# Hybrid encoder on one core: the first mixer's instruction order rewritten, M1 built on VectorE, states kept in x's words

## Chip, cores and metric

The kernel is written by hand in Bass and runs on one core of a Trainium2 chip. The metric is the device time of one execution in microseconds (us). Every buffer's place, every semaphore and the order of the instructions on each engine stand in the program; no scheduler changes them. A program on one core has one instruction stream for each of TensorE (PE), VectorE (DVE), ScalarE (ACT), GpSimd (POOL) and SyncE (SP); SP issues most DMAs.

## The reference

An encoder of two layers on x of 512 tokens by 1024 features, float32. Each layer is `x += mixer(RMSNorm(x)); x += HierMoE(RMSNorm(x))`. The change touches the mixer of layer 0, which runs two head groups from one input projection:

```python
z = (h @ w_in)
q, k, v, g, u = jnp.split(z, [512, 1024, 1536, 2048], axis=-1)
...
r = bidirectional_retention(q, k, v, decay_logit)      # 4 heads of 128, chunks of 128
...
y_ret = jax.nn.silu(g) * group_norm(r)
y_s5 = s5_glu(u, a_re, a_im, log_step, b_re, b_im, c_re, c_im, d_skip, w_glu, b_glu)
return jnp.concatenate([y_ret, y_s5], axis=-1) @ w_out
```

`s5_glu` is a diagonal state space in both directions: 32 channel groups of 16 channels, each with 64 complex states. For each group and direction, x_t = lambda x_(t-1) + B u_t, then y = d u + Re(C x) summed over the directions; then y = gelu(y), and y times sigmoid(y @ w_glu + b_glu). The mixer of layer 1 is windowed attention. HierMoE picks two of 32 experts for each token; each expert's weights are 6 MB, and all 32 are loaded in each layer.

## The kernel before

**Buffers.** `ring` has six slots of 4096 words a partition. In the expert stages slots 0 to 2 and 3 to 5 hold gate, up and down of two experts by turns; in the first mixer they hold pieces of `w_in`, tables of the state model (slots 3 to 5, from `V0`), the Toeplitz operand `TQ` (slot 1), the transposed operands `T4` of the retention (slot 2), and at the end the halves of `w_out`. `WK` ("work") holds q, k, v, g, u and small arrays, `HT` the normed input transposed and later scratch, `X` ("x_sb") the residual. PSUM has eight banks.

**The state model without a scan over tokens.** The 512 tokens are 64 chunks of 8 (`T8`, `NK`). `dve_s5_params` (L1107) computes lambda and its powers, `dve_s5_tables` (L1176) C times the powers of lambda and B for the convolution kernel inside a chunk, `dve_phasors` (L1207) the 64 powers of lambda^8's phase, by doubling: n values times the n-th power give the next n, and after each doubling that power is squared. `pool_m1` (L1382) multiplies, on GpSimd, B by powers of lambda for a quarter q of the groups (`M1`, 128 x 2048). `pe_m1` and `act_m1` transpose it to `W1S`, `pe_inc` (L1415) makes the chunk increments from it and u, `act_inc` copies them to SBUF, and `dve_states` (L1441) rotates them by the phasors, runs two scans over the 64 chunks, rotates back and writes the states of the quarter. `pe_y` (L1477) adds, in PSUM, the Toeplitz product inside the chunk and C times the states; `act_gelu` evacuates. All products of complex numbers go through `cmul` (L984 to L1000), six instructions each.

**Order in the program** (one sequence an engine, written out in `pe_mixer0` L1525, `act_mixer0` L1653, `dve_mixer0` L1717, `sp_mixer0` L1774). TensorE: norm transposes, u (64 x 512 for each of 8 token phases), transposes of C and of u, `z_block` (L1551) for q, k and g in four banks, kernel products (L1588), v, then the whole retention `pe_ret` (L1272), then `pe_m1`, `pe_inc`, `pe_y` interleaved by quarters, transposes of y (L1613), GLU products (L1624) with the transposes of the retention result between them, output projection (L1641, L1645). VectorE: `dve_small_logs` (L1055, decay logarithms and the masks of the retention), parameters, tables, phasors, `dve_kernel` (L1225), `dve_rotary` (L1240), `dve_ret`, four `dve_states`, `dve_gn` (L1354), the rest. GpSimd: small loads, then the four `pool_m1` behind `z_mm` 12. SP: x, pieces of `w_in`, small loads (s5_d in one transfer, L1785), the kernel stored to DRAM and loaded as `TQ` (L1812), `w_out`, and then `sp_moe` (L819), which loads expert weights as slots come free; its first loads wait for `yr_rdy`, `gl_mm`, and `o_mm` 4 and 8 (the output projection's halves).

## Time and profile before

| what | us |
|---|---|
| median of 3 runs (lowest, highest) | 1731.51 (1729.74, 1734.15) |
| the profiled execution: its time, its span | 1726.8, 1725.0 |
| TensorE busy | 1407.0 (82%) |
| VectorE busy | 539.9 (31%) |
| ScalarE busy | 246.3 (14%) |
| GpSimd busy | 230.0 (13%) |
| HBM read, written | 465.92 MB, 23.59 MB |

Busy time is summed over the span. The pages' slices are equal parts of the span, 43 us each; the stage tables below give the same by stretches of my choosing. In the timelines the first number is the start, the second the duration, and in brackets stands how long the engine sat idle before and who released it.

### The profile page before, as it was taken

The numbers are of one execution on the slowest core, as the hardware profiler recorded it, in microseconds if no ns is written. First come the engines' busy times: TensorE is split into PE (matmuls) and PEld (weight loads), VectorE is DVE, ScalarE is ACT, GpSimd is POOL, SyncE is SP. The second block draws the span as 40 slices with busy tenths as digits, with TensorE's granted clock in tenths as the row PEclk, the third lists the DMA queues.
The fourth block names the chain that finished last, engine by engine and source line by source line (L and its number), as shares of the span: only waits on it lengthen the run. The fifth ranks groups of instructions, "written<-read, shape, count | busy, mean of one in ns | idle before, by whom it ended". The sixth has DMA issues, their size and how long they took to land. (4 is left out here: it accounts for less than half of the span.)

```text
span 1725.0 us, 18834 instructions
## 1 busy us (share of the span) xinstructions
PE 1407.0 (82%) x7013; PEld 686.9 (40%) x7013; DVE 539.9 (31%) x1251; ACT 246.3 (14%) x529; POOL 230.0 (13%) x330
## 2 busy tenths in 40 slices
PE   7998746997988878878884988896997887887882
PEld 4444645555333333333332356544433333333330
DVE  6998589123111111110114039524111011011014
ACT  3101222111100000000011027412000000000001
POOL 0007070001111111111100000001111111111110
PEclk9999977996998998998996989996999999899896
DMA  7210502536999999999996110426999999999994
GB/s 241 71 52 21 45 13 84 213 151 236 365 397 411 404 410 412 407 406 409 400 407 248 54 49 2 195 85 228 341 384 410 408 407 406 409 405 411 406 419 160
DMA packets 70724, 473.49 MB, mean 274 GB/s; under 512 B 16676, under 2 KB 23556, under 8 KB 45968
## 3 DMA queue, kind: packets, MB, share of 16 engines
q1 hardware_dynamic: 57872, 448.07, 66.5%
q0 software_dynamic: 11376, 19.83, 3.5%
q10 hardware_dynamic: 1424, 4.89, 0.7%
q8 instruction: 34, 0.56, 0.1%
q14 instruction: 18, 0.15, 0.0%
HBM read 465.92 MB, written 23.59 MB: 284 GB/s over the span
## 5 line engine op out<-in xcount | busy, mean ns | idle before, releaser
L616 PE MATMUL psum<-ring,work 128*64 128x512 f32 x992 | 494.1, 656 | 117.2 <-DMA ring<-in_moe_w_up 115.7
L617 PE MATMUL psum<-ring,work 128*64 128x512 f32 x992 | 494.9, 657 | 0.0
L616 PEld LDWEIGHTS psum<-ring,work 128*64 128x64 f32 x992 | 144.9, 151 | 430.8 <-issue 427.1
L629 PE MATMUL psum<-ring,work 128*64 128x512 f32 x992 | 226.5, 598 | 31.1 <-DVE work L761 31.1
L758 DVE TENSOR_TENSOR work<-work,psum 64x512 f32<-64x512 f32 x64 | 44.2, 690 | 597.2 <-ACT work L722 597.1
L722 ACT ACTIVATE work<-psum 64x512 f32<-64x512 f32 x64 | 37.8, 590 | 833.6 <-PE psum L617 833.6
L617 PEld LDWEIGHTS psum<-ring,work 128*64 128x64 f32 x992 | 144.7, 151 | 2.5 <-issue 1.0
L629 PEld LDWEIGHTS psum<-ring,work 128*64 128x64 f32 x992 | 66.6, 136 | 144.9 <-issue 125.1
L764 DVE COPY work<-psum 128x512 f32<-128x512 f32 x64 | 44.2, 691 | 247.7 <-PE psum L629 247.7
L1562 PE MATMUL psum<-ring,hT 128*128 128x512 f32 x256 | 112.1, 600 | 2.1 <-ACT work L1685 2.1
L902 POOL COPY ints<-ints 64x1 uint32 (+1 forms) x64 | 11.4, 178 | 538.3 <-PE psum L608 499.4
L1562 PEld LDWEIGHTS psum<-ring,hT 128*128 128x128 f32 x256 | 49.1, 193 | 63.7 <-issue 63.7
L920 POOL DMA_INDIRECT y_dram<-work,ints x64 | 65.3, 1020 | 56.7 <-POOL ints L926 55.6
L909 POOL DMA_INDIRECT work<-h_dram,ints x64 | 61.8, 966 | 58.2 <-POOL ints L902 54.2
L608 PE MATMUL psum<-consts,work 64*128 64x64 f32 x512 | 67.3, 273 | 2.8 <-DMA work<-h_dram,ints 2.8
L608 PEld LDWEIGHTS psum<-consts,work 64*128 64x128 f32 x512 | 62.7, 204 | 4.7 <-DMA work<-h_dram,ints 3.1
L1934 PE MATMUL psum<-ring,hT 128*128 128x512 f32 x128 | 55.6, 593 | 0.7 <-ACT hT L1971 0.7
L622 PEld LDWEIGHTS psum<-consts,work 64*128 64x128 f32 x256 | 35.4, 209 | 51.9 <-issue 51.9
L1853 PE MATMUL psum<-hT,ring 128*64 128x512 f32 x256 | 55.2, 592 | 0.8 <-issue 0.8
L312 PE MATMUL psum<-consts,work 128*128 128x128 f32 x128 | 25.7, 367 | 33.4 <-DVE work L281 33.4
L719 ACT COPY work<-psum 128x512 f32<-128x512 f32 x64 | 37.4, 585 | 75.9 <-PE psum L608 75.9
L622 PE MATMUL psum<-consts,work 64*128 64x64 f32 x256 | 44.1, 292 | 0.0
(362 smaller groups left out, 1450.9 us busy)
## 6 DMA issues: line engine op xcount, KB each, us to landing
ring<-in_moe_w_gate SPq DMA_DIRECT2D x62, 2048.0 KB, 17.5
ring<-in_moe_w_up SPq DMA_DIRECT2D x62, 2048.0 KB, 22.9
ring<-in_moe_w_down SPq DMA_DIRECT2D x62, 2048.0 KB, 23.3
ring<-in_hyb_w_in SPq DMA_DIRECT2D x5, 2048.0 KB, 8.6
work<-y_dram SPq DMA_DIRECT2D x16, 512.0 KB, 7.2
ring<-in_swa_w_qkv SPq DMA_DIRECT2D x3, 2048.0 KB, 15.0
ring<-in_hyb_w_out SPq DMA_DIRECT2D x4, 1024.0 KB, 8.7
h_dram<-work ACTq DMA_DIRECT2D x8, 512.0 KB, 2.6
```

The source lines that it names most:

```text
L608: i = nc.tensor.transpose(bank[b][:, c * BLK:(c + 1) * BLK], XG[b][:, c::KC], ident[0:BLK, 0:BLK])
L616: nc.tensor.matmul(bank[2 + b][0:BLK, :], XT[b][:, c, :], g[:, c, :], start=c == 0, stop=c == KC - 1)
L617: i = nc.tensor.matmul(bank[2 + b][BLK:P, :], XT[b][:, c, :], u[:, c, :], start=c == 0, stop=c == KC - 1)
L622: i = nc.tensor.transpose(bank[4 + b][:, c * BLK:(c + 1) * BLK], HD[b][:, c::HC], ident[0:BLK, 0:BLK])
L629: i = nc.tensor.matmul(bank[6 + b][BLK * hf:BLK * (hf + 1), :], HTE[b][:, c, :], d[:, c, hf * HALF:(hf + 1) * HALF], start=c == 0, stop=c ...
L758: nc.vector.tensor_tensor(HD[b], AA[b], bank[2 + b][BLK:P, :], ALU.mult).then_inc(done, 1)
L764: nc.vector.tensor_copy(YE[b], bank[6 + b][:, :]).then_inc(done, 1)
L909: pool.indirect_dma_start(XG[b], None, h_dram, bass.IndirectOffsetOnAxis(STG[b], 0), bounds_check=S - 1, oob_is_err=False).then_inc(done, 16)
L920: pool.indirect_dma_start(y_dram, bass.IndirectOffsetOnAxis(SSTG[b], 0), YE[b], None, bounds_check=4 * S - 1, oob_is_err=False).then_inc(d ...
L1562: x = nc.tensor.matmul(bank[i % 4], hT[:, c, t * P:(t + 1) * P], w[:, c, :], start=c == 0, stop=c == KC - 1)
L1853: x = nc.tensor.matmul(bank[i][64 * hf:64 * hf + 64, :], w[:, c, 64 * (2 * k + hf):64 * (2 * k + hf) + 64], hT[:, c, :], start=c == 0, sto ...
L1934: x = nc.tensor.matmul(b, hT[:, c, t * P:(t + 1) * P], wo[n][:, c, :], start=c == 0, stop=c == KC - 1)
```

## The change

It rewrites the order of the first mixer on all engines, and with it:

- M1 is built on VectorE (`dve_m1`, in place of `pool_m1`), two quarters right behind the parameters and two later; quarter 0 lies in WK, the others in slot 0, and `W1S` in slot 0 too.
- Transposes of M1 (by halves, in banks 2 and 3), increments and kernel products stand between the tiles of q, k, v, g, which use two banks instead of four; v comes before g.
- `act_inc` is gone: VectorE reads the increments from PSUM. The states of all four quarters are kept, in the words of x (`XS`), so x is loaded a second time from DRAM before the output projection adds to it.
- `dve_phasors` takes the n-th power from the table itself, so the six squarings fall away. Small logs move behind the last states.
- y runs after all states in one stretch, ahead of the retention; the retention stands behind y, and the GLU products behind it, before the transposes of the retention result.
- Channel groups g and g + 16 share the two halves of the partitions, instead of 2j and 2j + 1. So `YT` has 128 rows and its transposes are 64 products with a quarter of the identity, s5_d comes in eight small loads, the parameter rows on GpSimd's queue in six instead of three.
- The expert weights' first loads wait for the same points, with other slots: slots 3 to 5 at `yr_rdy`, 0 at `gl_mm`, 1 and 2 at the projection's halves.

The core of the diff:

```diff
-        T4 = W(2, 2048, 2048)
-        M1 = [W(0, 2048 * b, 2048) for b in range(2)]
-        W1S = cut(WK, 4096, 2048)
+        T4, YT = W(2, 0, 2048), W(2, 2048, 2048)
+        M1 = [cut(WK, 2048, 2048)] + [W(0, 0, 2048)] * (NQ - 1)
+        W1S = W(0, 2048, 2048)
...
+        XS = [[cut(X, 1024 * q + 512 * i, 512) for i in range(2)] for q in range(NQ)]
...
             while n < NK:
-                bc = [ins_dim(m(x), 2, n) for x in ("qr", "qi")]
-                cmul(V, p3[0][:, :, n:2 * n], p3[1][:, :, n:2 * n], p3[0][:, :, 0:n], p3[1][:, :, 0:n], bc[0], bc[1],
-                     shp(cut(RR, 0, 32 * n), 32, n), shp(cut(RR, 1024, 32 * n), 32, n))
-                cmul(V, m("t3"), m("t4"), m("qr"), m("qi"), m("qr"), m("qi"), m("t1"), m("t2"))
-                V(tv.tensor_copy(m("qr", 2), m("t3", 2)))
-                V.sync()
+                w = min(n, NK - 1 - n)
+                bc = [ins_dim(x[:, :, n], 2, w) for x in p3]
+                cmul(V, p3[0][:, :, n + 1:n + 1 + w], p3[1][:, :, n + 1:n + 1 + w], p3[0][:, :, 1:1 + w], p3[1][:, :, 1:1 + w],
+                     bc[0], bc[1], shp(cut(RR, 0, 32 * w), 32, w), shp(cut(RR, 1024, 32 * w), 32, w))
                 n *= 2
...
-        def pool_m1(pool, V, q):
+        def dve_m1(dve, V, q):
 
             if q == 0:
-                pool.wait_ge(z_mm.s, 12)
-            elif q > 1:
-                pool.wait_ge(m1_tr.s, 4 * (q - 1))
+                dve.wait_ge(b_in, B_LOADS)
+            elif q == 1:
+                dve.wait_ge(u_mm.s, 4)
+            else:
+                dve.wait_ge(m1_tr.s, 4 * q)
...
         def dve_states(dve, V, q):
 
-            dve.wait_ge(inc_ev.s, 2 * q + 2)
-            if q >= 2:
-                dve.wait_ge(y_mm.s, 2 * (q - 1))
+            dve.wait_ge(inc_mm.s, 2 * q + 2)
...
+            def kernel_products():
+                pe.wait_ge(k_tab.s, 1)
+                pe.wait_ge(m1_ev.s, 8)
...
+            z_tile(0)
+            pe_m1(pe, 0, 0)
+            z_tile(1)
+            pe_m1(pe, 0, 1)
+            z_tile(2)
+            pe_inc(pe, 0)
...
+            z_tile(6)
+            kernel_products()
+            z_tile(7)
...
+            z_tile(15)
...
             for q in range(NQ):
+                pe_y(pe, q)
...
+            pe_ret_transposes(pe, 0)
             pe.wait_ge(y_ge.s, 2 * NQ)
             for mm in range(4):
                 for t in range(T8):
-                    x = nc.tensor.transpose(bank[4 + mm][:, t * 64:(t + 1) * 64], YT[:, 512 * t + mm:512 * t + 512:4],
-                                            ident[0:64, 0:64])
+                    for gg in range(2):
+                        rows = slice(64 * gg, 64 * gg + 64)
+                        x = nc.tensor.matmul(bank[4 + mm][rows, t * 64:(t + 1) * 64], YT[rows, 256 * t + mm:256 * t + 256:4],
+                                             ident[rows, rows], start=True, stop=True)
...
+            dve_s5_params(dve, V)
+            dve_m1(dve, V, 0)
+            dve_m1(dve, V, 1)
+            dve_phasors(dve, V)
+            dve_s5_tables(dve, V)
+            dve_states(dve, V, 0)
+            dve_kernel(dve, V)
+            dve_m1(dve, V, 2)
+            dve_states(dve, V, 1)
+            dve_m1(dve, V, 3)
+            dve_states(dve, V, 2)
+            dve_rotary(dve, V)
+            dve_states(dve, V, 3)
             dve_small_logs(V)
...
+            for j in range(QJ):
+                for gg in range(2):
+                    r0 = 32 * j + 16 * gg
+                    sp.dma_start(SMP[r0:r0 + GC, 4:8], bass.AP(A["s5_d"].tensor, 256 * gg + GC * j, [[1, GC], [QJ * GC, NQ], [1, 1]]),
+                                 allow_slow_non_contiguous=True).then_inc(b_in, 16)
...
             sp.wait_ge(y_mm.s, 2 * NQ)
+            for t in range(NT):
+                sp.dma_start(xv[:, t, :], A["x"][0, t * P:(t + 1) * P, :]).then_inc(x_in[t], 16)
+            wout(0)
+            sp.wait_ge(ym_tr.s, 4)
+            sp.wait_ge(r_o.s, RH)
+            wout(1)
```

How the order moves. TensorE around the kernel products, before (`s5_tables` is raised by VectorE behind the tables, `z_evac` by ScalarE; L1562 is a tile of q, k, g or v):

```order
L1562 MATMUL psum<-ring,hT 128x512 [waits z_evac]
L1562 MATMUL psum<-ring,hT 128x512 x7
L1588 MATMUL psum<-ring,work 32x128 [waits s5_tables,u_ready]
L1588 MATMUL psum<-ring,work 32x128 x63
L1562 MATMUL psum<-ring,hT 128x512 [waits z_evac,w_loaded1]
L1562 MATMUL psum<-ring,hT 128x512 x7
```

and now (L1569 is a tile, L1593 the kernel products, L1416 a half of M1's transposes):

```order
L1569 MATMUL psum<-ring,hT 128x512 [waits z_evac]
L1569 MATMUL psum<-ring,hT 128x512 x7
L1593 MATMUL psum<-ring,work 32x128 [waits s5_m1_evac,s5_tables]
L1593 MATMUL psum<-ring,work 32x128 x63
L1569 MATMUL psum<-ring,hT 128x512 [waits z_evac]
L1569 MATMUL psum<-ring,hT 128x512 x7
L1569 MATMUL psum<-ring,hT 128x512 [waits z_evac,w_loaded1]
L1569 MATMUL psum<-ring,hT 128x512 x7
L1569 MATMUL psum<-ring,hT 128x512 [waits z_evac]
L1569 MATMUL psum<-ring,hT 128x512 x7
L1416 MATMUL psum<-consts,ring 128x128 [waits s5_m1_evac,s5_kernel_ready,s5_m1]
L1416 MATMUL psum<-consts,ring 128x128 x7
```

Before, twelve tiles stood ahead of the kernel products; now seven do, and transposes of M1 stand between the tiles behind them.

TensorE behind the last tile, before (L1281 are the retention's transposes):

```order
L1562 MATMUL psum<-ring,hT 128x512 [waits z_evac]
L1562 MATMUL psum<-ring,hT 128x512 x7
L1281 MATMUL psum<-consts,work 128x128 [waits ret_scaled,z_evac,s5_kernel_ready]
L1281 MATMUL psum<-consts,work 128x128 x3
L1281 MATMUL psum<-consts,hT 128x128 x8
```

and now (L1630 the bias row for layer 1, L1498 the Toeplitz product of y, L1504 its product with the states):

```order
L1569 MATMUL psum<-ring,hT 128x512 [waits z_evac]
L1569 MATMUL psum<-ring,hT 128x512 x7
L1630 MATMUL psum<-work 16x512 [waits s5_m1_evac,attn_small_loaded]
L1498 MATMUL psum<-ring,work 64x128 [waits s5_toeplitz_loaded,s5_states]
L1498 MATMUL psum<-ring,work 64x128
L1504 MATMUL psum<-ring,x_sb 64x128 x8
```

y has taken the place of the retention, and its first product waits for the states of all quarters.

VectorE around the end of the tables, before (L1204 is the tables' last instruction, L1210 begins the phasors):

```order
L999 TENSOR_TENSOR ring<-work 128x576 [waits dve_steps]
L1204 MEMSET ring 128x32 [waits dve_steps]
L1210 MEMSET work 128x32 [waits u_transposed,s5_tables]
L1211 MEMSET work 128x32
L1212 COPY ring<-ring 128x32
```

and now (L1206 is the tables' last; what follows is the first state group):

```order
L1000 TENSOR_TENSOR ring<-work 128x576 [waits dve_steps]
L1206 MEMSET ring 128x32 [waits dve_steps]
L989 TENSOR_TENSOR work<-work,psum 128x512 [waits s5_inc,s5_tables]
L990 TENSOR_TENSOR work<-work,psum 128x512
L992 TENSOR_TENSOR work<-work 128x512 [waits dve_steps]
```

The phasors stand ahead of the tables now, and the states begin behind the tables, with PSUM as an input.

## Rows read from the trace of the kernel before

**Rows 1.** The page: DMA's busy tenths in 40 slices, and a group of matmuls.
```profile
DMA  7210502536999999999996110426999999999994
...
L616 PE MATMUL psum<-ring,work 128*64 128x512 f32 x992 | 494.1, 656 | 117.2 <-DMA ring<-in_moe_w_up 115.7
```
**Rows 2.** Stages: length; PE, PEld, DVE, ACT, POOL busy (instructions); clock, DMA share, GB/s.
```profile
20.03:38.78 18.75, 18.69 (x88) 8.94 (x90) 17.01 (x62) 2.32 (x4) 0.00 (x0) 1.00 0.72 191
38.78:63.10 24.32, 22.87 (x105) 11.59 (x102) 21.53 (x114) 7.60 (x13) 0.00 (x0) 0.93 0.31 108
63.10:108.50 45.40, 45.40 (x107) 20.14 (x106) 43.47 (x70) 3.55 (x6) 0.00 (x0) 1.00 0.13 47
108.50:135.20 26.70, 26.70 (x63) 11.78 (x62) 24.64 (x83) 0.60 (x1) 0.00 (x0) 1.00 0.12 40
135.20:145.06 9.86, 7.73 (x138) 5.13 (x137) 4.16 (x16) 3.35 (x5) 7.80 (x8) 1.00 0.01 2
145.06:176.55 31.49, 25.25 (x59) 10.83 (x57) 31.22 (x24) 2.34 (x4) 27.30 (x21) 0.98 0.27 40
181.80:212.65 30.85, 25.23 (x219) 24.47 (x218) 17.80 (x44) 7.00 (x15) 0.00 (x0) 0.99 0.43 34
217.35:242.95 25.60, 6.90 (x91) 6.12 (x89) 25.14 (x22) 1.92 (x4) 24.74 (x18) 0.68 0.00 1
259.50:270.86 11.36, 8.94 (x138) 6.96 (x135) 10.88 (x22) 2.95 (x6) 0.00 (x0) 0.80 0.04 13
283.50:298.50 15.00, 10.04 (x100) 8.12 (x101) 14.33 (x10) 3.96 (x5) 0.00 (x0) 0.73 0.41 142
302.30:321.20 18.90, 18.89 (x48) 12.05 (x49) 0.47 (x1) 4.00 (x7) 0.00 (x0) 0.84 0.87 365
```
**Rows 3.** Timeline of VectorE: start, us, instruction.
```profile
121.11 0.69 DVE L988 TENSOR_TENSOR work<-work,ring 128x512 f32<-128x512 f32 x1
...
125.21 0.19 DVE L988 TENSOR_TENSOR ring<-ring 128x32 f32<-128x32 f32 x1
...
126.55 1.23 DVE L988 TENSOR_TENSOR work<-work,ring 128x1024 f32<-128x1024 f32 x1
...
173.92 0.68 DVE L1252 TENSOR_TENSOR work<-work,consts 128x512 f32<-128x512 f32 x1
174.52 0.68 DVE L1253 TENSOR_TENSOR work<-work,consts 128x512 f32<-128x512 f32 x1
```
**Rows 4.** Timeline of GpSimd.
```profile
136.95 1.06 POOL L988 TENSOR_TENSOR norm_gain<-ring,work 128x512 f32<-128x512 f32 x1 [132.81 <-PE psum L1562]
...
171.86 1.59 POOL L999 TENSOR_TENSOR ring<-norm_gain 128x512 f32<-128x512 f32 x1
```
**Rows 5.** Timeline of TensorE.
```profile
52.41 84.35 PE L1562 MATMUL psum<-ring,hT 128*128 128x512 f32 x192
136.70 3.77 PE L1588 MATMUL psum<-ring,work 128*32 128x128 f32 x128
...
219.32 2.09 PE L1426 MATMUL psum<-work 128*64 128x64 f32 x64 [0.83 <-ACT work L1413]
230.94 3.67 PE L1403 MATMUL psum<-consts,ring 128*128 128x128 f32 x16 [9.53 <-POOL ring L999]
...
276.54 0.44 PE L1493 MATMUL psum<-ring,work 128*64 128x128 f32 x4
...
277.93 1.03 PE L1607 MATMUL psum<-work 32*16 32x512 f32 x2
...
296.08 4.10 PE L1613 MATMUL psum<-consts,work 64*128 64x64 f32 x32 [4.93 <-ACT work L1508]
```
**Rows 6.** Timeline of SP's DMA issues.
```profile
9.57 5.42 SPq L1785 DMA_DIRECT2D s_small<-in_s_d  x1
...
170.40 10.04 SPq L1812 DMA_DIRECT2D ring<-k_dram  x8
```
**Rows 7.** DMA issues by tile: count, KB each, median us to landing.
```profile
ring<-k_dram SPq DMA_DIRECT2D x8, 256.0 KB, 12.9
```

More of the change, by code:

```diff
@@ L43 @@
 NTAU = T8 + 1
+B_LOADS = 16 * 13
 AH = 16
@@ L817, in load_block_w, with sp_moe @@
             q.dma_start(W(3 * b + which), v).then_inc(done, 16)
-        def sp_moe(sp, l, free_s5, free_2, free_0, free_1, next_loads):
+        def sp_moe(sp, l, frees, next_loads):
             b0 = NE * l
-            for free, slots in ((free_s5, (3, 4, 5)), (free_2, (2,)), (free_0, (0,)), (free_1, (1,))):
+            for free, slots in frees:
                 free(sp)
@@ L1211, in dve_phasors @@
             V(tv.memset(p3[1][:, :, 0:1], 0.0))
-            V(tv.tensor_copy(m("qr"), m("e8r")))
-            V(tv.tensor_copy(m("qi"), m("e8i")))
+            for x, e8 in zip(p3, ("e8r", "e8i")):
+                V(tv.tensor_copy(x[:, :, 1], m(e8)))
             V.sync()
@@ new lines, in pe_mixer0 @@
+            z_tile(0)
[4 more added lines that the diff above has]
+            pe_inc(pe, 0)
+            pe_m1(pe, 1, 0)
+            z_tile(3)
+            pe_m1(pe, 1, 1)
+            z_tile(4)
+            pe_inc(pe, 1)
+            z_tile(5)
+            z_tile(6)
+            kernel_products()
+            z_tile(7)
+            z_tile(8)
+            z_tile(9)
+            pe_m1(pe, 2, 0)
+            z_tile(10)
+            pe_m1(pe, 2, 1)
@@ new lines, in pe_mixer0 @@
+            z_tile(11)
+            pe_inc(pe, 2)
+            z_tile(12)
+            pe_m1(pe, 3, 0)
+            z_tile(13)
+            pe_m1(pe, 3, 1)
+            z_tile(14)
+            pe_inc(pe, 3)
+            z_tile(15)
+            pe.wait_ge(a_in, 32)
+            pe.wait_ge(m1_ev.s, 4 * NQ)
+            nc.tensor.matmul(bank[3][0:AH, :], RB, OH[:, 0:S], start=True, stop=True).then_inc(f_mm.s, 1)
+            for q in range(NQ):
+                pe_y(pe, q)
+            pe.wait_ge(f_ev.s, 1)
@@ L1690, in act_mixer0, with z_out @@
[L1690 to L1705 removed]
+            def z_out(i):
+                _, reg = ZB[ZORD[i // NT]]
+                act.wait_ge(z_mm.s, i + 1)
+                if i == 2 * NT:
+                    act.wait_ge(k_mm.s, 2)
+                o = cut(WK, 2048 * reg + 512 * (i % NT), 512)
+                if ZORD[i // NT] == "g":
+                    A_(nc.scalar.activation(o, bank[i % 2], ACT.Silu), z_ev)
+                elif ZORD[i // NT] == "k":
+                    A_(nc.scalar.mul(o, bank[i % 2], RD ** -0.5), z_ev)
+                else:
+                    A_(nc.scalar.copy(o, bank[i % 2]), z_ev)
@@ new lines, in act_mixer0 @@
+            z_out(0)
+            act_m1(act, A_, 0, 0)
+            z_out(1)
+            act_m1(act, A_, 0, 1)
+            z_out(2)
+            act_m1(act, A_, 1, 0)
+            z_out(3)
+            act_m1(act, A_, 1, 1)
+            for i in range(4, 10):
+                z_out(i)
+            act_m1(act, A_, 2, 0)
+            z_out(10)
+            act_m1(act, A_, 2, 1)
+            z_out(11)
+            z_out(12)
+            act_m1(act, A_, 3, 0)
+            z_out(13)
+            act_m1(act, A_, 3, 1)
@@ L1706, in act_mixer0 @@
+            z_out(14)
+            act.wait_ge(k_st, 16)
+            act.dma_start(OH, A["c_band"]).then_inc(a_in, 16)
+            act.dma_start(RB, A["rel_bias"]).then_inc(a_in, 16)
+            z_out(15)
+            for q in range(NQ):
+                act_gelu(act, A_, q)
+            act_ret(act, A_)
+            act_gn(act, A_)
             for mm in range(4):
@@ L1709, in act_mixer0 @@
                    gl_sg)
-                if mm == 1:
-                    for m4 in range(4):
-                        act.wait_ge(yr_tr.s, m4 + 1)
-                        A_(nc.scalar.copy(YRT[:, 512 * m4:512 * m4 + 512], bank[4 + m4]), yr_ev)
+            for m4 in range(4):
+                act.wait_ge(yr_tr.s, m4 + 1)
+                A_(nc.scalar.copy(YRT[:, 512 * m4:512 * m4 + 512], bank[4 + m4]), yr_ev)
             act.wait_ge(f_ev.s, 1)
@@ L1762, in dve_add_out @@
                 dve.wait_ge(o_mm.s, 8 * l + i + 1)
+                if l == 0 and n == 0:
+                    dve.wait_ge(x_in[t], 32)
                 xx = xv[:, t, 512 * n:512 * n + 512]
```

335 lines of the change are left out of this document (139 added, 196 removed).

## The prediction

> **What bounds the kernel now.** I read the page first. Its slices [rows 1] show DMA at 0.9 for most of the span, in two long blocks, which are the two expert stages. There the matmuls of `pe_gu` (L616) wait 115.7 us in total for expert weights to land [rows 1]. Nothing in those stages changes except the order of the first loads, so their length stays. The blocks cannot start before the mixer ahead of each has ended, though: six ring slots hold the weights, and the mixer occupies them. In the first mixer's slices (the first nine) DMA stands at 0.0 to 0.5 after the start [rows 1]. So a microsecond taken from this mixer moves all that follows to the left by one. Its end for this purpose is the first output projection, which starts at 321.2 us, where the last stage of the table ends [rows 2].
>
> Within the mixer the stage table [rows 2] shows a relay. VectorE is full from 20 to 135 us (small logs 18.8, parameters 24.3, tables 45.4, phasors 26.7) while TensorE works on u, q, k, g. Then come rotary (31.5), retention (30.9), four groups of states, the group norm (15.0), and the GLU with the transposes of the retention result (18.9). From 176.5 us on TensorE and VectorE take turns. One thing stands out: the first group of states took 25.6 us and the third 11.4 for the same 22 instructions, and the rotary's 24 instructions took 31.2 us of VectorE. GpSimd was busy in just the slow ones (24.74 and 27.30 us, against 0.00) [rows 2]. An instruction on 128x512 takes 0.69 or 0.68 us when GpSimd is idle [rows 3]; the two at 173.92 and 174.52 follow right behind GpSimd's last one, which began at 171.86 and took 1.59 [rows 4]. The mean in the rotary was 31.22 / 24 = 1.30. The two engines slow each other.
>
> **The change, part by part.** I follow VectorE first, as it becomes the long chain. All durations are of the profiled execution.
>
> 1. Small logs leave the front: the parameters start at 20.0 instead of 38.8 and end at 20.0 + 24.3 = 44.3.
> 2. Matrix M1 moves from GpSimd to VectorE: per quarter two complex products, each of six instructions on 512 elements. One such product ran from 121.11 to 125.21, 4.1 us [rows 3], so 8.2 per quarter, 32.8 in all. Two quarters stand here: 60.7. The first waits for thirteen small loads, the second for u's matmuls; q's first tile, which stands behind those on TensorE, starts at 52.41 [rows 5], so the second doesn't wait.
> 3. Phasors lose six squarings with their copies, 126.55 - 125.21 = 1.34 each [rows 3], and one part in 32 of the last doubling (0.2): 26.7 - 8.2 = 18.5, to 79.2.
> 4. Tables 45.4: 124.6. Here TensorE waits (below).
> 5. State group 0: 11.4 [rows 2], now from PSUM instead of ScalarE's copy; same price, as no row shows more for PSUM. 136.0. The convolution kernel's 16 small instructions: 4.2, the busy time of their stage [rows 2]. 140.2. M1 of quarter 2: 148.4. State group 1: 159.8.
> 6. M1 of quarter 3 writes where TensorE still reads quarter 2, so it waits for that one's transposes, at about 162 by the count below: 170.2. State group 2 waits for its increments until about 171: 182.4.
> 7. Rotary without GpSimd beside it: 24 x 4.1 / 6 = 16.4 instead of 31.5. 198.8. State group 3: 210.2.
>
> So 190 us of VectorE, some 3 of them waits. Only M1 has no row of its own on VectorE. Bounds: below 29 (48 instructions at the 0.60 between the starts at 173.92 and 174.52 [rows 3]), above 51 (GpSimd's own 1.06 each [rows 4]). I take 32.8, from the row of the same engine and size.
>
> The Trainium skill (GPSIMD Engine Reference, Key points) calls VectorE structurally about twice as fast for elementwise work. By that, an estimate of mine, M1 would cost half of GpSimd's 51 us, 25, and the sum would be 7 us better. The rows give 0.68 against 1.06, a factor of 1.6, and the sum keeps to the rows.
>
> TensorE: the first tile starts at 52.4 as before. Twelve tiles took 84.35 us [rows 5], 7.0 each. Between them now stand sixteen transposes (half of 3.67 at full clock, 1.8) and the increment products (2.09) [rows 5] of two quarters, 8 together. After seven tiles it is at 52.4 + 49 + 8 = 109.5, where the kernel products wait for the tables: idle to 124.6, **15 us that were none before**. The wait costs nothing by itself, as VectorE is behind. But the clock falls: at 230.94, after 9.5 us idle, those transposes took 3.67 [rows 5]. So the kernel products at 3.77 [rows 5] or double, then a tile with a slow start: 139.5 after tile 7. Tiles 8 and 9, half the transposes, tile 10, the other half: 162, the time used in 6. Tiles 11 to 15 (35) with the transposes and increments of a quarter and the increments of the one before (6): 203. SP beside this: the Toeplitz loads go out behind tile 11, from 169, in 10 us [rows 6], and land 12.9 later in the median [rows 7]: by 197, before 210. w_glu, x again (2 MB) and half of w_out follow and are wanted only from 272, 297 and 290 on.
>
> Then all of y in one run: four quarters of four pieces. A piece took 277.93 - 276.54 = 1.39 at full clock [rows 5], a quarter 5.6, at half clock up to 11.1. With a slow start, 7.4 + 3 x 5.6 = 24.2: from 210.2 to 234.4. **Small logs, 18.8, stand beside it on VectorE** and end at 229.0; with the bias row and the first scaling, five instructions of at most 0.69, at 232.5: hidden, by 2 us. If y took less than 22, they would be next. Last GELU and the first head's transposes: 236. The transposes of y become 64 products instead of 32 transposes of 4.10 [rows 5]; by the increments, 32 such products in 2.09, 4.2 (bounds 2.1, and 8.4 at half clock). Last copy by VectorE: 241.2. Retention from its first increments on 30.9 [rows 2]: 272.1. Group norm 15.0: 287.1. The GLU's products (with a few transposes 18.9 [rows 2]) now run beside it, from 271.5 to 286 or 290. Last, transposes of the result 1.8 and a copy, with hand-over: 290.2. That is 321.2 - 290.2 = **31 us** earlier. ScalarE loses eight copies and has idle time everywhere; GpSimd only issues small loads.
>
> What follows (projection, router, expert stages) is equal: expert 0's gate loads earlier, but its up and down weights still wait for the projection's halves.
>
> The profiled execution's own time is 1726.8, the median 1731.51, 4.7 more: 1731.5 - 31 = **1700.5**.
>
> **The rivals.** (a) *TensorE stays slow after its waits.* This one ends on the other side. The new order cuts the projections with short transposes and waits. Where TensorE waited for VectorE between short groups, its granted clock was 0.68 (217 to 243) and 0.80 (259 to 271); with dense tiles it was 1.00 (63 to 108) [rows 2]. If it stayed at the lower level, 1.2 GHz, from 124.6 on, nine tiles would cost 7 us more each, 63, of which 7 are slack; y 17, retention and GLU some 10: 83 - 31 = 52 slower, 1783. It decides from about 38 us of slow work on, five tiles. Against it: between the short groups stand dense runs of 7 us. The Trainium skill (TensorE: Matmul & The Clock Gate, on oscillation) describes just this pattern, short groups between waits that start slow each time. A mild form, y alone slow, gives 1700.5 + 17 = 1717.5.
>
> (b) *The small loads block SP.* s5_d was one issue of 5.42 us [rows 6]; it is eight now, ahead of k's weights. At that price each they end 43 us after the B loads, near 70, land near 79, and VectorE's first M1 waits 34: 1734.5, no change. Against: that issue stood behind 4 MB of weights, and the eight together move as many elements.
>
> (c) *The slowness was not GpSimd's.* Then M1, rotary and states stay at 1.3 us an instruction: M1 +30, rotary +15, states +14: 1759.5. The rows at 173.92 and 174.52 [rows 3] speak plainly against it.
>
> (d) *It does not reach the end*, because the weight stream sets it: 1731.5. Against: DMA is hardly busy before the first block [rows 1].
>
> (e) Full clock and shorter waits everywhere: 40 us, 1691.5.
>
> **How the numbers follow.** Chances: forecast 0.76 (1693 to 1710), mild (a) 0.08, full (a) 0.05, (b) 0.04, (c) 0.02, (d) 0.01, (e) 0.04. Range 1687 to 1719: the forecast with M1's bounds (-4, +18), mild (a) and (e); 0.12 is left out. A difference of 0.3%, 5 us, is what a measurement here can tell from none. Faster 0.88, same 0.05, slower 0.07.
>
> **What would show it.** Right: no VectorE row on 128x512 much above 0.7 us in the mixer; the kernel products after a wait of 15 us near 125; the last state group done near 210; y in one run of about 24; the projection at 290, and expert stages of the old length. Wrong: granted clock near 0.5 in the tiles after 125 (a), a wait for the B loads at 44 (b), instructions of 1.3 us with GpSimd idle (c), longer expert stages (d).

## The result, and the profile after

The change made the kernel faster: 1701.13 us in the median of 4 runs (1697.05 to 1705.08), against 1730.62 (4 runs, 1728.84 to 1734.15) for the kernel before on the same chip. The ratio is 0.9833, with a 95% interval of 0.9812 to 0.9854. That is 29.5 us by the medians, or 1.7%, clear of the noise; 31 were forecast. The profiled execution took 1700.29 us, its span 1698.4.

The page of the changed kernel, to be held against [rows 1]: the slices of DMA's busy tenths, and the group of matmuls that waits for expert weights.

```profile
DMA  8012533458999999999984200436999999999994
...
L617 PE MATMUL psum<-ring,work 128*64 128x512 f32 x992 | 488.6, 650 | 120.3 <-DMA ring<-in_moe_w_up 118.9
```

The first long block is fuller at its front (8 where a 6 stood) and ends earlier (8 where the last 9 stood). The wait for weights is 118.9 us, 3.2 more than before: the expert stages did not shrink, they moved. From the first expert matmul to the end of the span it is 1316.0 us, and was 1314.8.

The stages of the changed kernel, in the columns of [rows 2]: M1 of quarters 0 and 1, phasors, tables, state group 0, kernel taps, M1 of quarter 2, rotary, y, y transposes, retention, group norm.

```profile
44.94:61.43 16.49, 15.04 (x84) 8.15 (x81) 15.88 (x25) 4.75 (x9) 0.00 (x0) 1.00 0.00 1
61.43:80.17 18.74, 18.74 (x116) 9.92 (x115) 17.63 (x41) 3.72 (x7) 0.00 (x0) 1.00 0.00 0
80.17:125.39 45.22, 31.63 (x146) 15.57 (x144) 43.47 (x71) 4.43 (x8) 0.00 (x0) 0.88 0.14 47
125.39:136.89 11.50, 11.37 (x143) 7.71 (x144) 10.95 (x23) 0.00 (x0) 0.00 (x0) 0.86 0.01 1
136.89:140.44 3.55, 3.55 (x10) 1.63 (x9) 3.24 (x16) 0.60 (x1) 0.00 (x0) 1.00 0.34 63
140.44:148.65 8.21, 8.21 (x20) 3.61 (x19) 7.93 (x12) 0.59 (x1) 0.27 (x1) 1.00 0.82 289
180.56:196.00 15.44, 15.44 (x102) 8.20 (x101) 15.16 (x25) 2.16 (x4) 0.00 (x0) 1.00 0.69 116
207.35:232.88 25.53, 25.53 (x337) 19.40 (x337) 19.45 (x66) 5.30 (x10) 0.53 (x1) 0.94 0.10 30
232.88:241.94 9.06, 7.89 (x129) 7.75 (x129) 4.39 (x4) 1.49 (x4) 0.00 (x0) 1.00 0.95 347
241.94:272.75 30.81, 25.16 (x210) 24.25 (x211) 17.80 (x44) 7.44 (x13) 0.00 (x0) 1.00 0.08 30
272.75:287.84 15.09, 13.13 (x31) 8.95 (x30) 14.36 (x10) 4.01 (x6) 0.00 (x0) 1.00 0.39 140
```

VectorE is full in every stage down to 207. The rotary, 31.49 us in [rows 2], takes 15.44, with GpSimd at 0.00. State group 0, 25.60 before, takes 11.50. M1 costs 8.2 us a quarter. Retention and group norm have kept their lengths.

Two of VectorE's waits, and then TensorE's, in the timeline of the changed kernel (in brackets: the idle time before the instruction, and who ended it):

```profile
160.32 0.69 DVE L989 TENSOR_TENSOR norm_gain<-ring,work 128x512 f32<-128x512 f32 x1 [0.37 <-PE psum L1416]
...
169.18 0.69 DVE L989 TENSOR_TENSOR work<-work,psum 128x512 f32<-128x512 f32 x1 [0.69 <-PE psum L1440]
```
```profile
125.53 5.24 PE L1593 MATMUL psum<-ring,work 128*32 128x128 f32 x128 [13.73 <-DVE ring L1206]
...
200.62 1.03 PE L1630 MATMUL psum<-work 32*16 32x512 f32 x2
207.35 0.69 PE L1498 MATMUL psum<-ring,work 128*64 128x128 f32 x4 [5.70 <-DVE x_sb L1476]
...
232.88 7.89 PE L1642 MATMUL psum<-consts,ring 64*64 64x64 f32 x128
...
291.42 5.87 PE L1670 MATMUL psum<-ring,work 128*128 128x512 f32 x8 [0.68 <-ACT work L1751]
```

Up to y, TensorE waits for VectorE (13.73 and 5.70 us) and VectorE almost never for TensorE. The output projection starts at 291.42, 29.8 us before 321.2 [rows 2].

### The profile page after: what moved, and what is told of

It is laid out like the page before. It is cut to its first block and busy times, and to the rows that moved or that the text cites. A ratio compares the mean times of both kernels' runs of the same rounds, so it can differ in the third digit from the quotient of the medians.

```text
span 1698.4 us, 18976 instructions
## 1 busy us (share of the span) xinstructions
PE 1399.7 (82%) x7109; PEld 670.4 (39%) x7109; DVE 531.7 (31%) x1257; ACT 240.9 (14%) x520; POOL 165.5 (10%) x285
## 5 line engine op out<-in xcount | busy, mean ns | idle before, releaser
L617 PE MATMUL psum<-ring,work 128*64 128x512 f32 x992 | 488.6, 650 | 120.3 <-DMA ring<-in_moe_w_up 118.9
L1569 PE MATMUL psum<-ring,hT 128*128 128x512 f32 x256 | 112.5, 594 | 0.0
L1569 PEld LDWEIGHTS psum<-ring,hT 128*128 128x128 f32 x256 | 47.6, 190 | 55.5 <-issue 55.2
L903 POOL COPY ints<-ints 64x1 uint32 (+1 forms) x64 | 11.4, 178 | 533.5 <-PE psum L609 494.7
```

Source lines behind the costliest of these rows:

```text
L617: nc.tensor.matmul(bank[2 + b][0:BLK, :], XT[b][:, c, :], g[:, c, :], start=c == 0, stop=c == KC - 1)
L1569: x = nc.tensor.matmul(bank[i % 2], hT[:, c, t * P:(t + 1) * P], w[:, c, :], start=c == 0, stop=c == KC - 1)
```

## The experiments

Each was timed beside the kernel before on its own chip, so ratios carry over from chip to chip better than times. The changed kernel's is 0.9833, and 0.001 of a ratio is 1.7 us. Where a difference of medians and one of ratios disagree, both are given.

### 1. Is VectorE's list the path? The small logs back in front

```diff
             V.sync()
+            dve_small_logs(V)
             dve_s5_params(dve, V)
...
             dve_states(dve, V, 3)
-            dve_small_logs(V)
```

> The changed kernel with one block moved back: the small logs (decays, router mask, softplus and the scaling of the keys, 18.8 us of VectorE in the changed kernel's trace) stand ahead of the state model's parameters again. Theory (VectorE's list is the chain from the start to the retention, and the small logs are hidden beside the products of the state outputs y): every later step moves back by 18.8 us and nothing is won behind y, so about 1720 us, +18.8. Rival (TensorE and the weight loads set the end of the stage, VectorE has slack after the change): between 0 and +12 us, the latter where only the 14 us wait of TensorE at the kernel products absorbs it.

1719.81 us, ratio 0.9942 (0.9923 to 0.9960): 18.7 above the changed kernel. VectorE's last group before the retention and its next instruction in this kernel's timeline:

```profile
226.60 1.67 DVE L1268 TENSOR_SCALAR hT<-work,ring 128x512 f32<-128x512 f32 x4
...
253.56 1.10 DVE L1783 COPY work<-psum 128x512 f32<-128x512 f32 x1 [25.28 <-PE psum L1642]
```

VectorE now sits idle for 25.28 us beside y, where the small logs had been. The whole price of this block is hidden in the change, and it is paid in full in front. The 13.73 us that TensorE had waited absorbed nothing.

### 2. The squarings, back in the changed kernel and out of the one before

In the changed kernel (with the two copies that start qr and qi; the result is used by nothing):

```diff
                      bc[0], bc[1], shp(cut(RR, 0, 32 * w), 32, w), shp(cut(RR, 1024, 32 * w), 32, w))
+                cmul(V, m("t3"), m("t4"), m("qr"), m("qi"), m("qr"), m("qi"), m("t1"), m("t2"))
+                V(tv.tensor_copy(m("qr", 2), m("t3", 2)))
+                V.sync()
                 n *= 2
```

> The changed kernel with the six squarings of the phasor loop and their copies put back on VectorE; their result is used by nothing, so this adds only their time (six of 1.34 us with the two copies, about 8 us). Theory (VectorE is the chain from the start on): +8 us, about 1709. Rival (VectorE has slack before the kernel tables, since TensorE's products wait anyway): 0.

1711.68 us, ratio 0.9886 (0.9847 to 0.9926): 10.6 above the changed kernel by the medians, 9.2 by the ratios, and the projection starts 9.1 later (300.55). In the kernel before, the new loop alone:

```diff
-                bc = [ins_dim(m(x), 2, n) for x in ("qr", "qi")]
-                cmul(V, p3[0][:, :, n:2 * n], p3[1][:, :, n:2 * n], p3[0][:, :, 0:n], p3[1][:, :, 0:n], bc[0], bc[1],
+                w = min(n, NK - 1 - n)
+                bc = [ins_dim(x[:, :, n], 2, w) for x in p3]
+                cmul(V, p3[0][:, :, n + 1:n + 1 + w], p3[1][:, :, n + 1:n + 1 + w], p3[0][:, :, 1:1 + w], p3[1][:, :, 1:1 + w],
...
-                cmul(V, m("t3"), m("t4"), m("qr"), m("qi"), m("qr"), m("qi"), m("t1"), m("t2"))
-                V(tv.tensor_copy(m("qr", 2), m("t3", 2)))
```

> The kernel before with one part of the change alone: the phasor loop without its squarings, about 8 us less of VectorE ahead of the kernel tables. Theory (before the change the same instructions lie on VectorE's path too, but it waits 5.4 us for the kernel products and for the first-mixer matrices that GpSimd makes behind it): the gain is between 0 and 3 us, since GpSimd's chain of matrices starts at the end of the tables' inputs and of the tile 12 projection and not of the tables. Rival (VectorE is the chain there as well): -8 us.

1730.26 us, ratio 1.0 (0.9979 to 1.0021): nothing. VectorE in this kernel, from its timeline:

```profile
126.38 1.19 DVE L999 TENSOR_TENSOR work<-work 128x992 f32<-128x992 f32 x1
140.94 0.29 DVE L1229 COPY work<-psum 128x128 f32<-128x128 f32 x1 [13.37 <-PE psum L1586]
```

It finishes 7.6 us earlier and then waits 13.37 us for the kernel products; in the kernel before that wait is 5.43. The same edit is worth its full price in the one order and nothing in the other.

### 3. Is M1 on GpSimd the cause of the slow VectorE?

M1 on VectorE, in the kernel before and its old order:

```diff
-                cmul(V, o[:, d, 0], o[:, d, 1], gg[0], gg[1], bb[0], bb[1], t1, t2, eng=nc.gpsimd,
+                cmul(V, o[:, d, 0], o[:, d, 1], gg[0], gg[1], bb[0], bb[1], t1, t2,
...
             dve_kernel(dve, V)
+            dve_m1(dve, V, 0)
+            dve_m1(dve, V, 1)
             dve_rotary(dve, V)
             dve_ret(dve, V)
+            dve_m1(dve, V, 2)
             dve_states(dve, V, 0)
+            dve_m1(dve, V, 3)
```

> The kernel before, in its old order, with the four quarters of the first-level matrices M1 computed by VectorE and not by GpSimd, and the loads of quarter 0's router ahead of nothing: GpSimd has no arithmetic left there. Theory (GpSimd and VectorE slow each other when both run float32 tensor-tensor work from SBUF: 1.5 us for an instruction of 0.69): VectorE pays 32.8 us for M1 and gets back the rotary's doubling (15.6 us), the states' doubling (about 11) and its waits for M1 (about 14), so -8 us, about 1722. Rival (GpSimd's M1 is free for VectorE, its slow instructions come from something else): +19 to +33 us, 1750 to 1763, with VectorE's rotary still at 1.5 us an instruction.

1722.99 us, ratio 0.9951 (0.9930 to 0.9973), 5.9 below its neighbour by the medians and 8.5 by the ratio. VectorE took 33 us of work over and the kernel still got faster. The rotary's stage, in the columns of [rows 2]:

```profile
162.95:178.52 15.57, 9.85 (x23) 3.99 (x22) 15.26 (x26) 1.17 (x2) 0.00 (x0) 0.88 0.35 36
```

This is 15.57 us against 31.49 [rows 2]. The rival wanted 19 to 33 us more.

The other way round, half of M1 back on GpSimd in the changed kernel:

```diff
-                cmul(V, o[:, d, 0], o[:, d, 1], gg[0], gg[1], bb[0], bb[1], t1, t2,
-                     done=m1_rdy if d else None)
+                cmul(V, o[:, d, 0], o[:, d, 1], gg[0], gg[1], bb[0], bb[1], t1, t2, eng=nc.gpsimd if on_pool else None,
+                     done=(m1_rdp if on_pool else m1_rdy) if d else None)
...
-            dve_m1(dve, V, 2)
             dve_states(dve, V, 1)
-            dve_m1(dve, V, 3)
```

> The changed kernel with the M1 matrices of quarters 2 and 3 computed by GpSimd again, beside VectorE's kernel, states 1 and 2 and rotary; quarters 0 and 1 stay on VectorE. Theory (the two engines slow each other): VectorE is rid of two quarters (16.4 us), GpSimd needs about 24 us for each of them, and VectorE's instructions beside it go from 0.69 to about 1.5 us, so the gain is given back: about +2 us against the changed kernel, 1699 to 1707. Rival (no slowing, GpSimd's work is free): -16 us, about 1685, with VectorE's instructions beside it still at 0.69 us.

1709.41 us, ratio 0.9906 (0.9879 to 0.9934): 8.3 above the changed kernel by the medians, 12.6 by the ratios, outside what either theory gave. Quarter 2 ran beside the tables. GpSimd there, and then on the same work while VectorE sat idle; below it VectorE:

```profile
91.11 1.66 POOL L993 TENSOR_TENSOR ring<-norm_gain 128x512 f32<-128x512 f32 x1
92.85 1.45 POOL L995 TENSOR_TENSOR norm_gain<-ring,work 128x512 f32<-128x512 f32 x1
...
171.91 1.26 POOL L993 TENSOR_TENSOR ring<-norm_gain 128x512 f32<-128x512 f32 x1
173.25 1.05 POOL L995 TENSOR_TENSOR norm_gain<-ring,work 128x512 f32<-128x512 f32 x1
```
```profile
86.37 0.76 DVE L993 TENSOR_TENSOR ring<-work 128x576 f32<-128x576 f32 x1
...
91.57 1.81 DVE L991 TENSOR_TENSOR work<-work,ring 128x576 f32<-128x576 f32 x1
...
109.29 0.75 DVE L991 TENSOR_TENSOR work<-work,ring 128x576 f32<-128x576 f32 x1
...
178.64 0.69 DVE L990 TENSOR_TENSOR work<-work,psum 128x512 f32<-128x512 f32 x1 [17.53 <-PE psum L1442]
```

The slowing is there, as expected: 0.76 becomes 1.5 to 1.8. What I had missed is the last row. The slowed tables end late, so the kernel products start at 134.89 for 125.53, and all that stands behind them on TensorE is 9.4 us late as well; the increments of quarter 2 reach VectorE at 178.64 for 169.18. VectorE has no M1 left to do until then, and the 16.4 us that it saved became a wait of 17.53. TensorE's list is the second chain, close behind the first.

The pure case: the changed kernel with 24 additions on GpSimd whose result nothing uses. The wait for them in the diff is met 21.6 us before VectorE gets there (202.78 against 224.40, below).

```diff
+            pool.wait_ge(m1_rdy.s, NQ)
+            for _ in range(24):
+                Q(nc.gpsimd.tensor_tensor(PM2, PM1, PM1, ALU.add), dum)
+                Q.sync()
             pool.wait_ge(r_sc.s, 1)
...
             dve_states(dve, V, 3)
+            dve.wait_ge(dum.s, 24)
             dve_small_logs(V)
```

> The changed kernel, and on GpSimd 24 additions of 128x512 float32 in SBUF, whose result nothing uses, from the end of the last M1 quarter on: they lie beside VectorE's states of quarter 2 (the first four of whose six long multiplications read one operand from PSUM) and its rotary (24 instructions with both operands in SBUF). Nothing waits for them. Theory (the two engines slow each other whenever both work from SBUF alone): GpSimd needs about 1.5 us for each while VectorE works from SBUF and about 1.1 where it doesn't, VectorE's rotary goes from 0.69 to about 1.5 us an instruction for as long as GpSimd runs, VectorE's instructions with a PSUM operand stay at 0.69 us; VectorE loses 10 to 15 us and the kernel with it, 1711 to 1716. Rival (the slowing of the kernel before came from GpSimd's DMA issues, from its waits or from the data's place and not from its arithmetic): 0, 1701.

1719.65 us, ratio 0.9950 (0.9934 to 0.9967): 18.5 above the changed kernel by the medians, 20.2 by the ratios, a little over the top of what was expected, for additions that no one needs. GpSimd and VectorE in this kernel:

```profile
169.56 33.22 POOL L2182 TENSOR_TENSOR norm_gain<-norm_gain 128x512 f32<-128x512 f32 x24 [17.88 <-DVE ring L1001]
```
```profile
172.29 0.69 DVE L995 TENSOR_TENSOR work<-work,psum 128x512 f32<-128x512 f32 x1
...
174.85 1.15 DVE L1455 COPY work<-ring 128x512 f32<-128x512 f32 x1
...
176.17 3.72 DVE L1460 TENSOR_TENSOR_SCAN work<-work 128x512 f32<-128x512 f32 x2
...
182.76 2.32 DVE L1479 TENSOR_TENSOR x_sb<-work 128x252 f32<-128x252 f32 x2
...
201.81 1.52 DVE L1253 TENSOR_TENSOR work<-work,consts 128x512 f32<-128x512 f32 x1
203.25 0.68 DVE L1254 TENSOR_TENSOR work<-work,consts 128x512 f32<-128x512 f32 x1
...
224.40 0.17 DVE L1063 TENSOR_SCALAR work<-s_small 128x8 f32<-128x8 f32 x1
```

GpSimd's last addition ends at 202.78, and VectorE's rotary drops from 1.52 to 0.68 us at once. The small logs begin at 224.40 instead of 207.40, 17.0 late. The row at 172.29 is as telling: with one operand in PSUM the instruction took its 0.69 us beside a working GpSimd. Those with all data in SBUF paid, also the copy with its one operand (1.15 for 0.43), the two scans (3.72 for 2.34) and a pair on 252 elements (2.32 for 0.75), which is why the sum passed my 10 to 15.

The Trainium skill (SBUF — State Buffer, A bandwidth-pool intuition that's wrong (but worth ruling out)) says that GpSimd and a VectorE operation that uses both of its ports can't work at the same time: one fully blocks. The trace agrees that they collide; that an operand in PSUM escapes is what the rows above show. Each engine's instruction gets longer: GpSimd's from 1.05 to 1.45 and from 1.26 to 1.66, VectorE's from 0.69 to 1.52. Whether one stands still within its row while the other works, durations can't tell. If the whole of each took turns, a pair would need 0.69 + 1.05 = 1.74 us; here VectorE started an instruction every 1.44 us (201.81 to 203.25) beside GpSimd's 24 in 33.22, 1.38 each, so they overlap at least in part.

### 4. Does TensorE's new wait cost anything? The kernel products later

```diff
             z_tile(6)
-            kernel_products()
             z_tile(7)
             z_tile(8)
+            kernel_products()
             z_tile(9)
```

> The changed kernel with TensorE's kernel products behind the projections of tiles 7 and 8 and not ahead of them, so that the 13.7 us in which TensorE waits for VectorE's tables are filled with projections. Theory (TensorE's wait costs nothing, since the retention starts when VectorE's states and y are done): 0, within 2 us of the changed kernel's 1701. Rival (TensorE's list is a second chain nearly as long): a gain of several us, up to 14.

1700.56 us, ratio 0.9851 (0.9828 to 0.9874): no difference from the changed kernel that these can show. TensorE's two waits in this kernel:

```profile
148.79 1.97 PE L1416 MATMUL psum<-consts,ring 128*128 128x128 f32 x8 [11.97 <-DVE ring L1000]
207.12 0.69 PE L1498 MATMUL psum<-ring,work 128*64 128x128 f32 x4 [5.72 <-DVE x_sb L1476]
```

The wait has moved to the M1 transposes, 11.97 us long, and y starts at 207.12 instead of 207.35.

### 5. What made the y transposes twice as dear as forecast?

The 64 products read every fourth word of y. Here they read neighbours, so that other rows of y reach the GLU than the reference's; nothing else changes.

```diff
-                        x = nc.tensor.matmul(bank[4 + mm][rows, t * 64:(t + 1) * 64], YT[rows, 256 * t + mm:256 * t + 256:4],
+                        x = nc.tensor.matmul(bank[4 + mm][rows, t * 64:(t + 1) * 64], YT[rows, 256 * t + 64 * mm:256 * t + 64 * mm + 64],
```

> The changed kernel, in which the 64 products that transpose y read 64 neighbouring words of each row and not every fourth word (so other rows of y reach the GLU than the reference's; the count and the shape of everything stay). Theory (the step of four words in the stationary operand is why a product takes 123 ns here against 65 ns in the state increments): 64 products in about 4.2 us, VectorE's four copies of 1.1 us then set the pace, -2.5 to -3 us, 1698.5. Rival (the price is that of this shape, an identity against 64 words of 64 partitions, whatever the step): 7.9 us again, 1701.

1697.05 us, ratio 0.9783 (0.9756 to 0.9810), below the changed kernel by 4.1 in the medians and 8.7 by the ratios; 2.5 to 3 were expected. TensorE in this kernel, and then the line's weight loads in the changed one and in this one:

```profile
232.83 3.95 PE L1642 MATMUL psum<-consts,ring 64*64 64x64 f32 x128
238.04 0.94 PE L1292 MATMUL psum<-work,hT 128*128 128x128 f32 x6 [1.26 <-DVE work L1783]
```
```profile
L1642 PEld LDWEIGHTS psum<-consts,ring x128: 189/213/213, 232.9 to 240.4; 64*64 64x64 f32 x128
```
```profile
L1642 PEld LDWEIGHTS psum<-consts,ring x128: 129/135/135, 232.8 to 236.5; 64*64 64x64 f32 x128
```

3.95 us against 7.89, a load 135 ns against 213, and the retention starts 3.9 us earlier (238.04 for 241.94). The step was the price, not the shape. A step of two or of eight was not tried. The Trainium skill (SBUF — State Buffer, Door 1: The DMA port swizzle) states that SBUF delivers full bandwidth only with at least two accesses to each line of 16 bytes; a step of four float32 words makes one. The trace agrees with that sentence, though the page then counts a step of four float32 as free.

### 6. Better than both: the last states ahead of the rotary

Once VectorE is the path, what must precede y should come first, and the rotary, which only the retention needs, can lie beside y like the small logs.

```diff
-            dve_rotary(dve, V)
             dve_states(dve, V, 3)
+            dve_rotary(dve, V)
             dve_small_logs(V)
...
-            pe_m1(pe, 2, 0)
             z_tile(10)
+            pe_m1(pe, 2, 0)
             pe_m1(pe, 2, 1)
...
             pe_m1(pe, 3, 0)
-            z_tile(13)
             pe_m1(pe, 3, 1)
-            z_tile(14)
             pe_inc(pe, 3)
+            z_tile(13)
+            z_tile(14)
             z_tile(15)
...
-            pe.wait_ge(f_ev.s, 1)
-            pe.wait_ge(z_ev.s, 16)
-            pe_ret_transposes(pe, 0)
             pe.wait_ge(y_ge.s, 2 * NQ)
...
+            pe.wait_ge(f_ev.s, 1)
+            pe.wait_ge(z_ev.s, 16)
+            pe_ret_transposes(pe, 0)
             pe.wait_ge(ym_ev.s, 4)
```

The kernel products stand as in experiment 4, and ScalarE's list follows TensorE's.

> The changed kernel with the kernel products behind tiles 7 and 8, the M1 products of quarters 2 and 3 each in one piece (the last increments ahead of tile 13), the last quarter's states ahead of the rotary on VectorE, and the transposes of y ahead of the first retention transposes on TensorE: the 16 us of rotary then lie beside the products of the state outputs, as the small logs do, and the y transposes beside the rotary. Theory (the chain is VectorE's list up to the last state, then y, and VectorE idles 6.5 us plus four short waits behind the small logs): about -10 us, near 1691; the bound above is the sum of the idle time, the y chain itself (some 25 us from the last state) stays. Rival (the last states must wait for the last increments, which stand behind all projections that z of the rotary needs as well; the wait only moves): 0.

1687.87 us, ratio 0.9787 (0.9761 to 0.9814): 13 below the changed kernel by the medians, and 12.7 below experiment 4, which ran beside it, but 8 by the ratios; 10 were expected. The same kernel a second time, beside the last one of this series:

> The kernel with the states ahead of the rotary once more, unchanged, beside the other on the same chip, so that the two are compared without the difference between chips: 1688 us, a span of 1686 again, within 2 us.

1689.81 us, ratio 0.9754 (0.9727 to 0.9782). So the gain over the changed kernel is 8 to 14 us. The timelines of the first of the two show VectorE's copies of y without a wait between them, and TensorE reaching the y transposes and then the retention with hardly a pause:

```profile
225.74 1.68 DVE L1268 TENSOR_SCALAR hT<-work,ring 128x512 f32<-128x512 f32 x4
227.51 3.96 DVE L1783 COPY work<-psum 128x512 f32<-128x512 f32 x4
```
```profile
148.35 1.97 PE L1416 MATMUL psum<-consts,ring 128*128 128x128 f32 x8 [4.91 <-DVE ring L1000]
...
221.77 7.89 PE L1639 MATMUL psum<-consts,ring 64*64 64x64 f32 x128 [1.29 <-ACT ring L1514]
...
231.52 0.94 PE L1292 MATMUL psum<-work,hT 128*128 128x128 f32 x6
```

The retention starts at 231.52 instead of 241.94, and at 231.33 in the second timing. Both engines reach that point together, so two more edits went for both lists: tile 11 ahead of the M1 products of quarter 2, and the y copies on ScalarE.

```diff
-            pe_m1(pe, 2, 0)
-            pe_m1(pe, 2, 1)
             z_tile(11)
+            pe_m1(pe, 2, 0)
+            pe_m1(pe, 2, 1)
-            pe_inc(pe, 2)
             z_tile(12)
+            pe_inc(pe, 2)
...
-                V(tv.tensor_copy(dst, shp(bank[4 + mm], T8, NK)), ym_ev)
+                A_(nc.scalar.copy(dst, shp(bank[4 + mm], T8, NK)), ym_ev)
```

> The kernel with the states ahead of the rotary (1687.9 us), and two edits more: the M1 products of quarter 2 stand behind tile 11 and not tile 10, which fills TensorE's wait of 4.9 us, and the four copies of the transposed y are ScalarE's and not VectorE's. Theory (in that kernel TensorE and VectorE end at nearly the same time ahead of the retention, TensorE with the y transposes at 229.7 us and VectorE with the small logs and key scaling at 227.4 us, so that either edit alone would give nothing and both together about 2 us, since the small logs then set the start): 1685.5, -2 to -3 against it. Rival (one of the two is not on the path): 0.

1688.93 us, ratio 0.9761 (0.9738 to 0.9785), between the two timings of the kernel without these edits, and the retention starts at 232.02: nothing gained. The 4.91 us wait was filled and came back one quarter later:

```profile
168.24 1.97 PE L1416 MATMUL psum<-consts,ring 128*128 128x128 f32 x8 [6.39 <-DVE ring L1000]
```

So tile 13 was put ahead of that as well (`z_tile(13)` before `pe_m1(pe, 3, 0)`).

> The kernel with the states ahead of the rotary, tile 11 ahead of the M1 products of quarter 2 and the y copies on ScalarE (1688.9 us), and one edit more: tile 13 stands ahead of the M1 products of quarter 3, which fills the wait of 6.4 us into which the one of quarter 2 had moved. Theory (TensorE is the chain ahead of the retention now, VectorE idles 5.3 us there): the last projection ends some 5 us earlier, the retention starts when the key scaling at 227.4 us and one head's transposes are done, so -2.5 to -3 us, near 1686. Rival (the last increments come later than VectorE wants them at 179 us, so that the wait only moves again, to the last states): 0.

1687.71 us, ratio 0.9746 (0.9718 to 0.9774), and 2.1 by the medians below the repeat above, which ran beside it; the intervals of the two overlap almost wholly. TensorE was early at last, and then:

```profile
227.76 1.09 PE L1279 MATMUL psum<-consts,work 128*128 128x128 f32 x4 [3.82 <-DVE hT L1268]
228.64 1.91 PE L1279 MATMUL psum<-consts,hT 128*128 128x128 f32 x8
230.35 1.06 PE L1279 MATMUL psum<-consts,work 128*128 128x128 f32 x4
231.20 1.37 PE L1292 MATMUL psum<-work,hT 128*128 128x128 f32 x6
```

It waited 3.82 us for VectorE and started slow: the sixteen transposes took 3.44 us (227.76 to 231.20) instead of the 1.9 that they take without a wait (229.60 to 231.52 in the kernel above). The retention started at 231.20, 0.3 earlier. VectorE's list releases the transposes at 227.6 now, however early TensorE is.

The two timings of the one kernel show what a single profiled execution is worth. The first eight matmuls of its output projection, in the first and in the second:

```profile
280.28 3.70 PE L1670 MATMUL psum<-ring,work 128*128 128x512 f32 x8 [0.69 <-ACT work L1751]
```
```profile
280.71 5.94 PE L1670 MATMUL psum<-ring,work 128*128 128x512 f32 x8 [0.68 <-ACT work L1751]
```

TensorE had sat idle equally long ahead of them in both (1.97 us before the transposes of the result, 0.7 before the projection), but the granted clock over these matmuls was 1.00 in the one and 0.61 in the other. With the slow transposes ahead of them, the first expert matmul came at 368.69 and 371.81, 3.1 us apart, for the same program.

## Why the prediction was right, and where it was off

**The bound and the rates.** VectorE's list is the path from the start to y (experiments 1, 2, 4), and GpSimd's arithmetic made it slow before (experiment 3, three kernels). M1 at 8.2 us a quarter was measured at 8.2; tables 45.4 at 45.2; the rotary 16.4 at 15.4, since the 4.1 for six instructions that I had taken from a dependent chain was 3.86 in this one; state groups 11.4 at 11.3 to 11.5.

**Step by step.** The parameters ended at 44.9 (forecast 44.3), M1's first two quarters at 61.4 (60.7), phasors at 80.2 (79.2), tables at 125.4 (124.6), group 0 at 136.9 (136.0). The sixteen small instructions of the convolution kernel took 3.6 us for 4.2, so quarter 2 of M1 ended at 148.65 (148.4) and group 1 at 159.95 (159.8). The two waits of steps 6 and 7 came to 1.1 us instead of 3, as the transposes of quarter 2 were done at 160 and not 162. State group 2 began 1.8 us early by it, and with the rotary's 1.0 this ends the last group at 207.4 instead of 210.2: 2.8 us of luck.

**TensorE.** The new wait of 15 us was 13.73, and harmless. The clock fell there as the rows of before had shown: 0.88 over the tables' stage, and the kernel products took 5.24 us instead of 3.77. It was 1.00 again over the next tile (130.7 to 137.7), so rival (a) did not come; y ran from 207.35 to 230.98, 23.6 us for a forecast of 24.2. The price of y's wait is in its first pieces, 0.69 and 1.97 us for 0.44 and 1.09.

**The term that was mis-sized** is "by the increments, 32 such products in 2.09, 4.2" for the y transposes. They took 7.89. Increments read their stationary operand from neighbouring words, these in steps of four (experiment 5: 3.95 without the step). The upper bound of the text, 8.4, held, though it was drawn for another cause, the clock; the granted clock was 1.00 there. The nearer row stood in the kernel before: its transposes of y also read in steps of four, and took 4.10 / 32 = 128 ns each [rows 5], which gives 8.2 for 64. Their clock was 0.50, which may have hidden the other cause, but their weight loads, 217 ns at that clock, were as long as those of the changed kernel at 1.00 (213):

```profile
L1613 PEld LDWEIGHTS psum<-consts,work x32: 192/217/217, 296.1 to 299.8; 64*128 64x128 f32 x32
```

With VectorE's copies behind, the retention started at 241.9 (forecast 241.2): the two errors, 3.7 and -2.8, almost cancelled, which is luck. Without that luck the forecast would have stood 4 us off at one end or 3 at the other, still inside its range.

**Small logs.** They ended at 226.1 (229.0) and the first scaling at 228.6 (232.5), 2.4 us ahead of y's end for the 2 given: hidden. VectorE then idled 6.5 us until the first transposed y was there, and that room was the clue to experiment 6.

**The end.** Group norm ended at 287.8 (287.1), the projection started at 291.4 (290.2), 29.8 earlier. Behind it a piece was lost again: its first eight matmuls took 5.87 us for 3.60 before, and the first expert matmul came 27.8 us earlier (382.4 for 410.2). TensorE now waits for the group norm just ahead of them, as it did not before; but the wait alone does not decide it, since behind the same wait experiment 6 had 3.70 in one execution and 5.94 in another. In the eleven profiled executions with the new order these eight took 3.70 us four times and 5.50 to 6.16 seven times. Behind the first expert matmul the fourteen profiled executions took 1312 to 1320 us, in no order that follows the edits. So by the profiled executions the whole is 26.5, by the medians 29.5; a single execution is not a sum to be trusted to 3 us.

**Rivals (b), (c), (d).** The eight issues of s_d took 4.79 us together and M1 began at 44.94, right behind the parameters, so the order of the small loads cost nothing. No VectorE addition or product on 128x512 took more than 0.7 us between 20 and 240. The weight stream began with the projection, and what follows the first expert matmul was 1.2 us longer than before.

Not tried: the second load of x, the pairing of groups g and g + 16, and keeping the states in x's words were never undone alone. That they cost nothing is read from the trace only.

## What to carry to other kernels

Find the engine whose list is the path, then order that list by who waits: first what releases another engine's long run, last what only the stage after needs. A removed instruction is worth its full price on that list and nothing off it, and the same edit can be either, depending on the order around it. Before giving an idle engine some of the work, look at what the busy one's instructions read: where both work from SBUF, the help may cost more than it brings.

## What the runs showed of the hardware

- GpSimd arithmetic beside VectorE doubles VectorE's float32 instructions on 128x512 with all operands in SBUF (0.69 to 1.52 us) and triples those on 252 elements of a row (0.75 to 2.32 for two), while those with an operand in PSUM keep 0.69 us. GpSimd itself pays too (1.05 to 1.45, 1.26 to 1.66).
- A stationary operand of TensorE read in steps of four float32 words loads in 213 ns, one of neighbours in 135, and 64 products take 7.89 us against 3.95.
- Behind the same short waits of the same program TensorE's granted clock was 1.00 in one execution and 0.61 in another (eight matmuls in 3.70 or 5.94 us).
- Filling one engine's wait mostly moved it: 13.73 us at the kernel products became 11.97 at the M1 transposes; 4.91 at quarter 2 became 6.39 at quarter 3. Where a wait was left ahead of a short run, the slow start took back what had been won (transposes in 3.44 us for 1.9).
